# Two-layer hybrid decoder trunk: modulation products over 2048 columns, other slots for them, S5 scan and gate row in other places

## What is computed

```python
cs = jax.nn.silu(c)
for l in range(DEPTH):
    mod = (cs @ w_ada[l] + b_ada[l]).reshape(B, 6, D)
    sh1, sc1, gt1, sh2, sc2, gt2 = [mod[:, i][:, None, :] for i in range(6)]
    h = rmsnorm(x, g_pre_mix[l]) * (1.0 + sc1) + sh1
    y = hybrid_mixer(h, ...)       # mLSTM heads | S5 scan | sparse attention, then an output projection
    x = x + gt1 * rmsnorm(y, g_post_mix[l])
    h = rmsnorm(x, g_pre_ffn[l]) * (1.0 + sc2) + sh2
    y = conv_ffn(h, ...)           # gated MLP, width 5504
    x = x + gt2 * rmsnorm(y, g_post_ffn[l])
```

## Time and profile before

| | us |
|---|---|
| three runs: median (lowest, highest) | 2496.05 (2494.68, 2496.05) |
| the profiled execution | 2484.45 |
| its span, first to last instruction | 2482.7 |
| PE busy in it | 2358.0 (95%) |
| DVE busy | 1890.2 (76%) |
| ACT busy | 1309.1 (53%) |
| mean granted TensorE clock | 0.978 |

### The profile page before, as it was taken

How to read it: one execution, slowest core, us unless ns; L and a number is a source line. 1 busy time by engine, 2 the same in 40 slices (tenths; PEclk the granted TensorE clock), 3 DMA queues, 4 the chain that set the end, 5 groups by cost and what they waited for, 6 DMA issues and landing times.

```text
span 2482.7 us, 39930 instructions
## 1 busy us (share of the span) xinstructions
PE 2358.0 (95%) x13810; PEld 2061.2 (83%) x13810; DVE 1890.2 (76%) x2769; ACT 1309.1 (53%) x2138; POOL 226.7 (9%) x384
## 2 busy tenths in 40 slices
PE   5898998989999999999979999999899999999998
PEld 3788987778888888888869998887788888888887
DVE  7979988779999999766678877658897666665555
ACT  5265655555554554444468556554645545544444
POOL 1111111111111111000001030001010000000000
PEclk9899998999999999999989999999999999999999
DMA  9999778767999999788865765739596555556664
GB/s 388 400 337 330 281 253 265 263 268 275 353 338 331 341 340 349 238 289 271 277 232 172 249 217 187 204 128 347 175 365 214 190 190 187 192 188 189 194 194 161
DMA packets 197337, 643.04 MB, mean 259 GB/s; under 512 B 27281, under 2 KB 49937, under 8 KB 191457
## 3 DMA queue, kind: packets, MB, share of 16 engines
q1 hardware_dynamic: 125346, 421.72, 48.6%
q0 software_dynamic: 51264, 205.04, 23.5%
q10 hardware_dynamic: 20608, 14.72, 1.9%
HBM read 626.68 MB, written 14.71 MB: 258 GB/s over the span
## 4 chain that ended last, share of the span: by engine, by line
PE 73%; DVE 13%; DMA 8%; ACT 4%; issue 2%; SPq 1%; ACTq 0%; DVEq 0%; POOLq 0%
PE ps L1281 25%; PE ps L768 18%; PE ps L1282 13%; PE ps L751 6%; DMA ring<-stream 5%; DVE w_lo L1910 4%; PE ps L1154 3%; DVE mix L1910 2%; DVE ada_w L1916 2%; PE ps L825 2%; DMA ada_w<-ada_d 2%; ACT w_hi L1342 1%; DVE mix L1916 1%; DMA gate_rows<-gg 1%; DVE xs L1916 1%
## 5 line engine op out<-in xcount | busy, mean ns | idle before, releaser
L1910 DVE TENSOR_TENSOR w_lo<-ring,w_hi 128x1024 fp32r<-128x1024 f32 x720 | 882.1, 1228 | 476.6 <-ACT w_hi L1342 472.5
L1342 ACT ACTIVATE w_hi<-ring 128x1024 fp32r<-128x1024 f32 x720 | 762.5, 1059 | 802.3 <-PE ps L1282 341.4
L1281 PE MATMUL ps<-hT,w_hi 128*128 128x512 f32 x2688 | 931.9, 392 | 0.0
L1282 PE MATMUL ps<-hT,w_lo 128*128 128x256 f32 x2688 | 748.6, 279 | 0.0
L1281 PEld LDWEIGHTS ps<-hT,w_hi 128*128 128x128 f32 x2688 | 503.3, 187 | 113.6
L1282 PEld LDWEIGHTS ps<-hT,w_lo 128*128 128x128 f32 x2688 | 506.4, 188 | 0.0
L1916 DVE SCALAR_TENSOR_TENSOR ada_w<-ada_w,cs_row 128x1024 f32<-128x1024 f32 (+1 forms) x332 | 405.5, 1258 | 19.9 <-DMA ada_w<-ada_d 19.9
L751 PE MATMUL ps<-hT,w_hi 128*128 128x256 f32 x2176 | 415.4, 293 | 4.4 <-DVE w_lo L1910 4.2
L751 PEld LDWEIGHTS ps<-hT,w_hi 128*128 128x128 f32 x2176 | 349.8, 197 | 16.8 <-issue 15.7
L751 PE MATMUL ps<-hT,w_lo 128*128 128x256 f32 x1088 | 312.7, 287 | 0.0
L751 PEld LDWEIGHTS ps<-hT,w_lo 128*128 128x128 f32 x1088 | 214.1, 197 | 0.0
(11 more groups left out here) (316 smaller groups left out, 2425.7 us busy)
## 6 DMA issues: line engine op xcount, KB each, us to landing
ring<-stream SPq DMA_DIRECT2D x746, 512.0 KB, 4.6
ada_w<-ada_d POOLq DMA_DIRECT2D x320, 512.0 KB, 6.4
ada_w<-ada_d POOLq DMA_DIRECT2D x12, 1024.0 KB, 10.0
ada_lo<-ada_d POOLq DMA_DIRECT2D x10, 1024.0 KB, 13.7
ada_hi<-ada_d POOLq DMA_DIRECT2D x10, 1024.0 KB, 10.3
mix<-stream SPq DMA_DIRECT2D x14, 512.0 KB, 13.6
xs<-x SPq DMA_DIRECT2D x2, 2048.0 KB, 12.0
s_in_w<-mix ACTq DMA_DIRECT2D x8, 512.0 KB, 6.2
```

Of the source, the lines that this page charges most:

```text
L1281: pe.matmul(ps[:, bank, :], w_hi[:, s, ks], hT[:, k, :, :], start=k == 0, stop=False)
L1282: m = pe.matmul(ps[:, bank, SEQ:2 * SEQ], w_lo[:, s, ks], hT_hi[:, k, :], start=False, stop=k == KT - 1)
L1342: s.activation(w_hi[:, c % SPLIT, :], ring[:, at % RING, :], ACT.Copy).then_inc(hi_ready, 1)
L1910: return v.tensor_tensor(o, a, b, op)
```

## The change

A modulation product now takes two chunks, 2048 columns with one sum (`ada_pair`); a unit is 8 pairs (`APAIRS`), `ada_part` has one column for each, and `ada_finish` has one addition. The first pair of a unit waits for the end of the unit before it. POOL still loads chunks of 512 KB into four slots; a pair waits for two and frees two. The tables count pairs and differ: with pairs as two chunks, layer 0 is ahead of the old table by up to 5 chunks from tile 25 to 28 and level at the end, and layer 1 has pairs in slots 0, 16, 18 and 19 and none behind 33. In the slot, `s5_scan` stands before `rope`, and `weighted` directly behind the slot's first pair (behind `masked` where the slot has none), before the rest. On ACT, `gate_spread(1)` stands behind the first ten steps of the down loop, which are written out.

```diff
+APAIRS = ACH // 2
-ADA_TILE = ({11: 3, 12: 3, 13: 3, 14: 1, 15: 1, 16: 1, 17: 1, 18: 3, 19: 2, 20: 3, 21: 3, 22: 2, 23: 1, 24: 1, 25: 1, 26: 3,
-             27: 2, 28: 3, 29: 2, 30: 2, 31: 2, 32: 3, 33: 6, 34: 4, 35: 4, 36: 4, 37: 2, 38: 2, 39: 4},
-            {26: 3, 28: 1, 31: 1, 32: 1, 33: 4, 34: 3, 35: 3})
-ADA_PIECE = ([1] * 24, [0] * 6 + [1] * 16)
+ADA_TILE = ({11: 1, 12: 2, 13: 2, 15: 1, 17: 1, 18: 2, 19: 1, 20: 1, 21: 2, 22: 1, 23: 1, 24: 1, 25: 1, 26: 1, 27: 1, 28: 2, 30: 1, 31: 1, 32: 2, 33: 2, 34: 2, 35: 2, 36: 2, 38: 1, 39: 2},
+            {0: 1, 16: 1, 18: 1, 19: 1, 26: 2, 32: 1, 33: 1})
+ADA_PIECE = ([1, 0] * 12, [0] * 6 + [1, 0] * 8)
...
-                    ada_until(ada_share(l, k) + ASLOT)
+                    ada_until(2 * ada_share(l, k) + ASLOT)
...
-                with s.Fori(0, 4) as i:
+                for k in range(10):
+                    down(0, k)
+                gate_spread(1)
+                with s.Fori(1, 4) as i:
                     for k in range(10):
                         down(i, k)
                 down(4, 0, True)
-                gate_spread(1)
                 joint(1, l + 1, 0 if l < DEPTH - 1 else None)
...
-            def ada_chunk(u, j):
-
-                v.wait_ge(ada_full[j % ASLOT], (u - HEAD_UNITS) * (ACH // ASLOT * 16) + (16 * (j // ASLOT) + 16))
-                w = ada_w[:, j % ASLOT, :]
-                half = j % 2
-                stt(w, w, 1.0, cs_row[:, half * AW:(half + 1) * AW], ALU.mult, ALU.mult,
-                    ada_part[:, j // 2, half:half + 1]).then_inc(ada_step, 1)
+            def ada_pair(u, q):
+
+                a = 2 * q % ASLOT
+                if q == 0:
+                    v.wait_ge(mod_ready, u)
+                for h in range(2):
+                    v.wait_ge(ada_full[a + h], (u - HEAD_UNITS) * (ACH // ASLOT * 16) + (16 * (2 * q // ASLOT) + 16))
+                w = ada_w[:, a:a + 2, :].rearrange("p a b -> p (a b)")
+                stt(w, w, 1.0, cs_row[:, :], ALU.mult, ALU.mult, ada_part[:, q:q + 1]).then_inc(ada_step, 2)
 
             def ada_finish(u, col):
 
                 v.wait_ge(ada_step, u * ACH + ACH)
-                tt(col, ada_part[:, :, 0], ada_part[:, :, 1], ALU.add).then_inc(ada_sum, 1)
-                v.wait_ge(ada_sum, u + (1 - HEAD_UNITS))
                 b = ada_b_c[:, u * UG:(u + 1) * UG] if isinstance(u, int) else ada_b_c[:, bass.ds(u * UG, UG)]
-                tt(col, col, b, ALU.add).then_inc(mod_ready, 1)
+                tt(col, ada_part[:, :], b, ALU.add).then_inc(mod_ready, 1)
...
                     w_rest(2 * k + AHEAD + 1)
+                    if IN_TILE + 1 <= k < IN_TILE + 7:
+                        s5_scan(*divmod(k - IN_TILE - 1, 3))
                     if l == 0 and k in ROPE_V:
                         rope(ROPE_V.index(k))
...
                     if 0 <= k - ITEM_TILE < NI:
                         masked(k - ITEM_TILE)
+                        mixer_ada(min(ada_share(l, k - 1) + 1, ada_share(l, k)))
+                        weighted(k - ITEM_TILE)
                     mixer_ada(ada_share(l, k))
...
-                    if IN_TILE + 1 <= k < IN_TILE + 7:
-                        s5_scan(*divmod(k - IN_TILE - 1, 3))
-                    if 0 <= k - ITEM_TILE < NI:
-                        weighted(k - ITEM_TILE)
                     if k == ITEM_TILE + 2:
                         gate_chain()
...
-                            for j in range(4 * k, 4 * k + 4):
-                                ada_chunk(u, j)
+                            for q in range(2 * k, 2 * k + 2):
+                                ada_pair(u, q)
```

More of the change, by code:

```diff
@@ L179 @@
 for _l in range(DEPTH):
-    assert ada_share(_l, NT) + sum(ADA_PIECE[_l]) == (N_IN[_l] + N_OUT[_l]) * ACH and U_IN[_l] + N_IN[_l] == U_OUT[_l]
+    assert ada_share(_l, NT) + sum(ADA_PIECE[_l]) == (N_IN[_l] + N_OUT[_l]) * APAIRS and U_IN[_l] + N_IN[_l] == U_OUT[_l]
 A_OFF, _o = {}, 0
@@ L244, in trunk @@
         fold = sb("fold", [P, CW])
-        ada_part = sb("ada_part", [P, UG, 2])
+        ada_part = sb("ada_part", [P, UG])
         head_sum = sb("head_sum", [P, HEAD_UNITS * UG])
@@ L317, in trunk @@
         b_in, bias_tr, bias_ready = sem("b_in"), sem("bias_tr"), sem("bias_ready")
-        ada_step, ada_sum = sem("ada_step"), sem("ada_sum")
+        ada_step = sem("ada_step")
         mod_ready = sem("mod_ready")
@@ L2375, in mixer_ada @@
                     for j in range(ada_done[0], n):
-                        u = U_IN[l] + j // ACH
-                        ada_chunk(u, j % ACH)
-                        if j % ACH == ACH - 1:
+                        u = U_IN[l] + j // APAIRS
+                        ada_pair(u, j % APAIRS)
+                        if j % APAIRS == APAIRS - 1:
                             ada_finish(u, mod_col(u))
@@ L2585, in _ @@
                         down(i, k)
-                        for j in range(ACH * N_DOWN[l] * (10 * i + k) // 40, ACH * N_DOWN[l] * (10 * i + k + 1) // 40):
-                            u = U_DOWN[l] + j // ACH
-                            ada_chunk(u, j % ACH)
-                            if j % ACH == ACH - 1:
+                        for q in range(APAIRS * N_DOWN[l] * (10 * i + k) // 40, APAIRS * N_DOWN[l] * (10 * i + k + 1) // 40):
+                            u = U_DOWN[l] + q // APAIRS
+                            ada_pair(u, q % APAIRS)
+                            if q % APAIRS == APAIRS - 1:
                                 ada_finish(u, mod_col(u))
```

## The result

The changed kernel is **slower**: 2512.34 us median (2510.61 to 2518.16, seven runs) against 2496.05 (2491.73 to 2503.96, seven runs), ratio 1.0069, 95% interval 1.0047 to 1.0090, some 17 us. The forecast was 2481.1 us with a range of 2472 to 2492, so its sign was wrong and the time lies outside its range.

A forecast was written before the change was run, and what follows sets the result against it. PE bounds the up loop; room was seen in mixers and joints. Joints 4.9, layer 0's mixer 4.5 and layer 1's 5.5 sum to 14.9 us, taking 2496.05 to 2481.1 us, range 2472 to 2492.

The forecast's parts named there:

- Step 7: Output projection pieces, up and down loops, GpSimd's issues and ACT's ten unrolled steps: no effect on time.
- Step 2: One sum over 2048 columns: 0.08 us a pair; 3.0 us of DVE work in layer 0's mixer, nothing beside full PE.
- Step 3: Layer 0's mixer, new slots: slot 33's stall goes, 3.6 us gained; two chunks more ahead cost 2.3 us of DVE.
- 1, spread: Joints after the down loops: issuing the gate row's spread early gains 4.3 us in layer 0, 0.6 in layer 1.
- rival (d): Up loops: slots freed in pairs make loads late if landings average 8.9 us or more; 20 us lost, 2501; chance 0.07.
- Rival (c): Wide products in layer 0's mixer save the documentation page's whole fixed cost: 2.4 us more, 2478.7 us; chance 0.04.
- 4, weights earlier: Mixers, attention weights ahead of the second pair: PE gains 3.3 us in layer 0; DVE idles 4.5 us for exponentials.
- not under 6: Expected sign in the trace: PE's waits at line 1044 fall from 16.2 us to under 6.
- 5, scan: Slot 19, scan moved ahead of rope: PE's 3.2 us wait at line 893 goes in layer 0; nothing in layer 1.
- 6, layer 1's mixer: Layer 1's new slots: gate row's write lands in 13 to 16 us, not 19.0, gaining 5.5 us (2.5 to 8).

The follow-up runs named there:

- all but pairs: Kernel before with early gate-row spread, scan ahead of rope, weights behind the first two chunks and both new slot tables, in single chunks everywhere: 2485.90 us, ratio 0.9971.
- new slots alone: Kernel before with the new slot tables for both mixers, counted in single chunks, instruction order and pieces as before: 2492.59 us, ratio 0.9989.
- order alone: Kernel before with the scan ahead of rope and the attention weights behind the slot's first two chunks, single chunks, old slots: 2483.43 us, ratio 0.9954.
- order and spread: Kernel before with scan ahead of rope, weights behind the first two chunks and the early gate-row spread, single chunks, old slots: 2479.80 us, ratio 0.9947.
- twos: Kernel before with 1024-column products in up and down loops waited for and freed two at a time, no wide instruction there: 2502.32 us, ratio 1.0023.

## Why the prediction was wrong, point by point

Two steps failed above all. Step 7 put the output projections and the up loops at nothing; they cost 4 us each in the projections and 8.5 to 16 in the loops. Step 2 is behind it: it counted what a pair saves DVE and not what it does to the slots. Step 3 failed as well: a gain of 1.3 us came out as a loss of about 6.

**1, spread: right.** The first product of the joint of layer 0 waits for ACT's sum and not for the gate row:

```profile
1293.88 1.95 DVE L1912 TENSOR_TENSOR mix<-ps,mix 128x1024 f32<-128x1024 f32 x2 [1.37 <-ACT mix L1372]
...
1303.89 1.28 DVE L1918 SCALAR_TENSOR_TENSOR xs<-mix,stat,xs 128x1024 f32<-128x1024 f32 x1
```

244.9 to 240.8 us is 4.1 against the 4.3 forecast, 0.5 against 0.6 in layer 1. Nearly all that was forecast arrived, so nothing to speak of was lost in the down loop.

**2, the wide product: the instruction right, its cost incomplete.** The next one starts 2.21 us on (1801.51 to 1803.72 in layer 1's up loop), as forecast. What was missing is what the edit does to the slots: a pair needs its second chunk at once, where single products needed it 1.15 us later, and gives its first slot back 1.1 us later. I charged that in slot 35 (+1.0) and in rival (d) and nowhere else. In the mixer the first places were slots 12 and 13, where two pairs stand behind one another. With four single chunks in each (all but pairs) DVE waits 1.2 and 1.3 us in slot 12 and is done at 176.6; in slot 13 it doesn't wait (180.82 to 185.40). With pairs it waits 6.3 us and is done at 179.9, then 3.0 us and is done at 191.5. After, with PE's waits that follow:

```profile
177.64 2.29 DVE L1918 SCALAR_TENSOR_TENSOR ada_w<-ada_w,cs_row 128x2048 f32<-128x2048 f32 x1 [6.34 <-DMA ada_w<-ada_d]
...
181.22 0.77 PE L751 MATMUL ps<-hT,w_hi 128*128 128x256 f32 x2 [5.47 <-DVE w_lo L1912]
...
184.06 2.28 DVE L1918 SCALAR_TENSOR_TENSOR ada_w<-ada_w,cs_row 128x2048 f32<-128x2048 f32 x1
...
189.32 2.29 DVE L1918 SCALAR_TENSOR_TENSOR ada_w<-ada_w,cs_row 128x2048 f32<-128x2048 f32 x1 [2.97 <-DMA ada_w<-ada_d]
...
192.90 0.48 PE L751 MATMUL ps<-hT,w_hi 128*128 128x256 f32 x2 [2.00 <-DVE w_lo L1912]
```

PE stood still for 5.5 us (1.9 with single chunks), and behind it the granted clock was 0.55 from 180 to 185 us. From 150 to 205 us it was 0.91 where before had 1.00:

```profile
150.00:205.00 55.00, 46.36 (x409) 44.42 (x408) 37.55 (x38) 43.82 (x74) 5.24 (x10) 0.91 0.87 318
```

Rival (c) stays without support: 2.21 against 2 x 1.15 again gives 0.08 and not 0.157. The formula behind the 0.157, in the Trainium skill (VectorE: DVE Perf Modes, section on the TRN2 errata), is one for the duration of an fp32 tensor_tensor add; the durations here agree with it (1.22 and 2.29 us), the starts don't follow it. Either saving is small beside a wait of 3 us.

**3, slots of layer 0: wrong.** I took 3.6 us for the stall at slot 33, which did go (0.9 left), and paid 2.3 us for two chunks ahead at the end of it. The cost came earlier: with new slots alone, 4.4 us by the 10th chunk of the table above, behind slots 12 and 13 with four chunks each in place of three, and 9 by the 28th, where the table is up to 5 chunks ahead. In that trace PE waits longer for data of the ring of weights, the first time for the attention's compression. New slots alone, then before:

```profile
209.71 0.91 PE L926 MATMUL ps<-ring,side 128*32 128x128 f32 x16 [4.92 <-DMA ring<-stream]
```

```profile
205.92 0.65 PE L927 MATMUL ps<-ring,side 128*32 128x128 f32 x16 [2.02 <-DMA ring<-stream]
```

At 289.6 and 294.4 us it waits 2.1 and 2.8 us for S5's weights, where before had 1.4 and 0.4. I had counted DVE's time alone. Why these loads come later there isn't shown.

**4, weights earlier: right in slot 34 and in layer 1, undone by the pair in slot 34.** In single chunks PE's wait at line 1044 in slot 34 is 2.1 us in all three kernels with the new order and the old slots of layer 0, and 4.4 in the seven with the old order. In layer 1 the waits fell from 5.7 to 7.3 us to 3.2 and 3.9. The size forecast for layer 0, 3.3, came out in order alone (9.6 to 6.3) by luck: order and spread, with the same mixer, has 12.5, and over all traces the mean fell from 12.1 to 9.3. In the changed kernel both layers have 13.1 us and not under 6, 9.0 of them in layer 0: the pair in front of `weighted` itself waited for data in slot 34,

```profile
384.79 2.29 DVE L1918 SCALAR_TENSOR_TENSOR ada_w<-ada_w,cs_row 128x2048 f32<-128x2048 f32 x1 [3.80 <-DMA ada_w<-ada_d]
...
387.21 0.16 DVE L1912 TENSOR_TENSOR att_s<-att_s,gates_t 128x4 f32<-128x4 f32 x1
```

and the weights with it, so that PE's wait there was 4.6 us (3.8, 2.3 and 6.8 in the other kernels with pairs in these slots). I had placed this cost behind the weights and not ahead of them. The waits for the exponentials came, 5.1 us against the 4.5 forecast.

**5, scan: right in layer 0, and a new wait in layer 1.** PE's wait at line 893 is 0.6 us in layer 0 (3.2). But the changed kernel has one of 2.6 us in layer 1, where before has none, so the wait isn't gone but moved. It comes with layer 1's new slots (0.9 to 2.8 us in all eight traces that have them, none in the nine without). GpSimd waits for the pair in slot 18 before it issues the next loads and, behind them, does its part of rope. That now falls beside the two `w_lo` ahead of the scan. After, DVE, GpSimd and PE's wait:

```profile
1457.15 2.28 DVE L1918 SCALAR_TENSOR_TENSOR ada_w<-ada_w,cs_row 128x2048 f32<-128x2048 f32 x1
...
1460.74 6.21 DVE L1912 TENSOR_TENSOR w_lo<-ring,w_hi 128x1024 fp32r<-128x1024 f32 x2 [1.29 <-ACT w_hi L1342]
```

```profile
1460.00 1.04 POOL L670 DMA_DIRECT2D ada_w<-ada_d  x2 [15.13 <-DVE ada_w L1918]
1461.06 1.30 POOL L661 TENSOR_TENSOR side<-side,rope_s 128x512 f32<-128x512 f32 x1
```

```profile
PE ps L893 <- DVE mix L1912: 2.6, 1, 2.6
```

The two `w_lo` take 6.21 us, where two take 2.35 at 1473.48. In layer 1's mixer no `w_lo` away from GpSimd's rope took over 1.23 us in any trace; beside it they took up to 4.0.

Order with all its costs, in single chunks, is worth 11.5 us, above what steps 4 and 5 summed to.

**6, layer 1's mixer: the mechanism right, the gain not.** The gate row's write landed after 15.2 us, inside the 13 to 16 forecast (19.0; 15.7 to 18.6 in the six others with old slots and old order), and with the order alone after 11.9. But the mixer gained 3.6 us against this one trace of before, which at 355.3 is the longest of those kernels (351.4 to 353.9 in the six others). I had priced the step on one execution's waits. The order gives this gain without the slots, and the slots bring nothing: what they take from the waits at line 1044 comes back at line 893. Layer 0's write of the gate row, which I didn't look at, took 19.4 to 22.3 us in the four traces with pairs in the new slots and 12.1 to 16.1 in the others; what that cost isn't separated.

**7, "nothing": wrong, and the largest term.** The projections cost 4 us each, in lumps (1.4 and 1.9) and late data. The up loops are rival (d), by its mechanism but not by its number. I let it decide from a mean landing of 8.9 us, and the median here is 6.0, the longest 10.4 (from 560 to 800 us), so by that test it shouldn't have come. But the loads of a step aren't averaged: one that takes over 7.5 us holds DVE then and there, and one that lands early gives nothing back. 17.7 us of such waits in layer 0 reach PE as 3.0 us, since `w_lo` has four chunks ready. No row of before could show what may come on top: behind a stall PE can go on at its slower pace, for all the rest of the loop. Of the 12 runs with pairs in the loops alone the lowest is 17 us above the lowest of before and the highest 4 us above the highest, as if runs with both loops at the faster pace were missing. That stalls favour the slower pace isn't shown.

In sum: pairs in the loops cost 8.5 us (alone), pairs outside them about 8, new slots about 6 against order and spread alone; order and spread give 13 back. That makes some 10 us slower, against 12 to 17 measured. Each term is uncertain by 5 us or so, and the loops' pairs came out at 11 to 16 beside the rest of the change.

**Open.** What sets PE's pace at a loop's start and at a stall isn't known. In 22 up loops without a stall the step from couple to couple was 0.3467 us in 11 and 0.3533 in 11, and never changed inside a stretch. In the eight loops with pairs or twos and stalls (the change twice, two kernels of the loops alone), 21% of the couples of products were at 0.3467, which would make (0.50 - 0.21) x 8.9 = 2.6 us a loop. The stalls themselves (a loop's length less its steps at their own pace) are 3.1 us a loop in the mean, 6 for two loops; with the pace it would be 11. Both lie in the interval of the 8.5 us (4 to 13), so the time doesn't decide whether the pace belongs to the cost. Six last stretches out of eight at the slower pace may be chance.

## What to carry to other kernels

- To join two buffers' work is, for the loads, almost to halve the number of buffers: count the time left to the last load of a pair, at each place, and compare it with the longest landings of the trace and not with their mean. Where it falls short, set the same pairs further apart: five of the six up loops with pairs over five steps had no stall of PE.
- A wait costs at the place where it stands in the order: put nothing that may wait for a DMA in front of what another engine is waiting for. Where work is moved to idle time of its engine, look at who waits for it there: GpSimd's rope came later by it, beside DVE's work ahead of the scan.
- Before pricing a step on one trace's waits, ask for a second trace; here one stage differed by 4 us and one loop by 9 between executions of the same code.

## What the hardware showed that was not expected

With the granted clock at 1.00 and PE never idle, the same loop of products runs at 0.3467 or 0.3533 us a couple (1.9%, 8.9 us a loop). The pace was kept from a loop's start to its end where nothing stalled, and it changed, if at all, only across a gap of PE, some of them under 0.1 us (order and spread, 674.8 us). It can account for most of the 20 to 25 us between runs of one kernel. Neither the granted clock nor a wait shows it, only the count of instructions in a stretch.

A stall also costs more than its own time when it is long: behind 6.45 us of standing still the granted clock fell and took 1.9 us more, behind stalls of up to 1.7 us in such loops it didn't fall.

DVE's `w_lo` is slower beside GpSimd's rope: up to 4.0 us in place of 1.22. Why is shown by no run here.
